# A router's softmax: one division for all eight heads at the end, and its loop of heads written out

## The reference, cut to what matters

```
sv, si = lax.top_k(s, PEER_TOPK)                       # 16 best of 128 keys, two halves per head
cand = sv[:, :, 0, :, None] + sv[:, :, 1, None, :]     # 256 candidate sums
cidx = si[:, :, 0, :, None] * N_KEYS + si[:, :, 1, None, :]
fv, fi = lax.top_k(cand.reshape(t, PEER_HEADS, 256), PEER_TOPK)
e = jnp.take_along_axis(cidx.reshape(t, PEER_HEADS, 256), fi, axis=-1)
g = jax.nn.softmax(fv, axis=-1)                        # over the 16 picks of a head
a = jax.nn.gelu(jnp.einsum('thkd,td->thk', peer_u[e], hb))
return jnp.einsum('thk,thkd->td', g * a, peer_v[e])
```

## Time and profile before

| what | us |
|---|---|
| three runs | 4075.23, 4058.43, 4070.72 |
| their median | 4070.72 |
| the profiled execution | 4065.13 |
| its span in the trace | 4063.3 |
| early router, VectorE's heads to its end | about 337 to 528 |
| late router, VectorE's heads to its end | about 1930 to 2238 |

### The profile page before, as it was taken

One profiled execution on the slowest core, in us unless ns is written; L12 is line 12 of the kernel. 1 busy time (PEld: TensorE's weight loads), 2 busy tenths in 40 slices (PEclk: granted clock), 3 DMA queues, 4 the chain that ended last, 5 costly groups with the idle time before them and its releaser, 6 DMA issues. The chain is left out here.

```text
span 4063.3 us, 57177 instructions
## 1 busy us (share of the span) xinstructions
PE 3284.5 (81%) x19892; PEld 2772.6 (68%) x19892; DVE 3008.0 (74%) x5897; ACT 1042.9 (26%) x1915; POOL 1648.1 (41%) x1320
## 2 busy tenths in 40 slices
PE   7665548787689889675663776999999999999997
PEld 4435424455455555334663666999999999999997
DVE  3316968678576777374998996888888888888886
ACT  2211112223122222111110553222232222222321
POOL 0004535346555655264455773333323333333232
PEclk9577779667787888777776888999999999999998
DMA  3032158468798887586100236888878888788786
GB/s 116 8 129 86 31 206 286 155 215 276 268 319 276 294 291 245 206 321 234 32 26 1 117 149 247 276 275 277 282 270 278 286 278 274 274 276 279 276 277 219
DMA packets 303822, 876.75 MB, mean 216 GB/s; under 512 B 34009, under 2 KB 125450, under 8 KB 292554
## 3 DMA queue, kind: packets, MB, share of 16 engines
q0 software_dynamic: 147456, 536.94, 39.0%
q1 hardware_dynamic: 154170, 334.15, 22.7%
q10 hardware_dynamic: 2016, 3.67, 0.2%
HBM read 819.17 MB, written 55.74 MB: 215 GB/s over the span
## 5 line engine op out<-in xcount | busy, mean ns | idle before, releaser
L109 POOL DMA_INDIRECT x_got<-v,x_expert x512 | 562.4, 1098 | 1062.9 <-DVE x_y L130 541.1
L109 POOL DMA_INDIRECT x_got<-u_rows,x_expert x512 | 613.8, 1199 | 659.8 <-DVE x_y L130 294.7
L130 DVE SCALAR_TENSOR_TENSOR x_y<-x_got,x_hidden,x_y 128x1024 f32<-128x1024 f32 x512 | 656.1, 1281 | 40.5 <-DMA x_got<-v,x_expert 38.0
L123 DVE SCALAR_TENSOR_TENSOR x_got<-x_got,x_y 128x1024 f32<-128x1024 f32 x512 | 626.7, 1237 | 43.8 <-DMA x_got<-u_rows,x_expert 42.2
L1667 PE MATMUL e_a<-h2h,e_uh 128*128 128x272 f32 x2048 | 590.4, 288 | 19.4 <-DVE e_ul L1745 19.4
L1669 PE MATMUL e_a<-h2h,e_ul 128*128 128x272 f32 x2048 | 594.0, 290 | 0.0
L1684 PE MATMUL e_y<-e_wh,e_vh 128*128 128x272 f32 x2048 | 588.9, 288 | 3.0 <-DVE e_wl L1768 3.0
L1668 PE MATMUL e_a<-h2l,e_uh 128*128 128x272 f32 x2048 | 589.2, 288 | 0.0
L1685 PE MATMUL e_y<-e_wl,e_vh 128*128 128x272 f32 x2048 | 588.7, 287 | 0.0
L1686 PE MATMUL e_y<-e_wh,e_vl 128*128 128x272 f32 x2048 | 587.7, 287 | 0.0
L1667 PEld LDWEIGHTS e_a<-h2h,e_uh 128*128 128x128 f32 x2048 | 386.3, 189 | 19.6 <-issue 19.6
(11 more groups left out here) (376 smaller groups left out, 5805.4 us busy)
## 6 DMA issues: line engine op xcount, KB each, us to landing
e_u<-uT SPq DMA_DIRECT2D x128, 512.0 KB
e_v<-v SPq DMA_DIRECT2D x64, 1024.0 KB
gates_d<-g_stage SPq DMA_DIRECT2D x8, 4352.0 KB
e_gate<-gates_d SPq DMA_DIRECT2D x32, 1088.0 KB
d_page<-page SPq DMA_DIRECT2D x128, 144.0 KB
d_latent<-page_rows SPq DMA_DIRECT2D x128, 128.0 KB
t0r_w<-w_pq SPq DMA_DIRECT2D x16, 512.0 KB
x_got<-u_rows,x_expert POOLq DMA_INDIRECT x512, 5.8
```

Of the source, the lines that this page charges most:

```text
L109: pool.indirect_dma_start(out=self.got[n % RING_G][:], out_offset=None, in_=self.tables[phase], in_offset=bass.IndirectOffsetOnAxis(ap=sel ...
L123: dve.scalar_tensor_tensor(out=row[:], in0=row[:], scalar=1.0, in1=self.y[g][:], op0=ALU.mult, op1=ALU.mult, accum_out=self.hidden[:, g, k ...
L130: dve.scalar_tensor_tensor(out=self.y[g][:], in0=row[:], scalar=self.hidden[:, g, k:k + 1], in1=self.y[g][:], op0=ALU.mult, op1=ALU.add).t ...
```

## The change

The exponentials go straight into their columns of `out[:, 0]` instead of back into `gate`. VectorE's `tail` of a head keeps only the sum, written to the head's column of a sum tile for all heads. The reciprocal and the product are done once, behind the last head, over all heads: 48 sums and 128x768 elements in the late router, 24 and 128x384 in the early one. The wait before L1446 is for the exponentials of the head before instead of its product; the waits for `c_gate` count to 1 instead of 8. In `heads` the hardware loop is replaced by a Python loop, so that each engine but SyncE has the code of all eight heads written out.

```diff
-        tot = sb("c_tot", [P, T])
-        inv = sb("c_inv", [P, T])
+        tot = sb("c_tot", [P, T, H])
...
             first(0, 0, None, False)
-            with eng.Fori(0, H // 2 - 1) as i:
-                first(2 * i + 1, 1, tail(2 * i, 0), False)
-                first(2 * i + 2, 0, tail(2 * i + 1, 1), False)
-            first(H - 1, 1, tail(H - 2, 0), True)
+            for m in range(1, H):
+                first(m, m % 2, tail(m - 1, (m - 1) % 2), m == H - 1)
             tail(H - 1, 1)()
...
-                    pe.wait_ge(s["c_gate"], H)
+                    pe.wait_ge(s["c_gate"], 1)
...
-                    act.activation(gate[:], gate[:], ACT.Exp).then_inc(s["c_exp"], 1)
+                    act.activation(out[:, 0, :, m * TOPK:(m + 1) * TOPK], gate[:], ACT.Exp).then_inc(s["c_exp"], 1)
...
-                after(dve, s["c_gate"], m)
+                after(dve, s["c_exp"], m)
...
                 dve.wait_ge(s["c_exp"], m + 1)
-                dve.tensor_reduce(tot[:], gate[:], AX, ALU.add).then_inc(s["c_tot"], 1)
-                dve.wait_ge(s["c_tot"], m + 1)
-                dve.reciprocal(inv[:], tot[:]).then_inc(s["c_inv"], 1)
-                dve.wait_ge(s["c_inv"], m + 1)
-                dve.tensor_tensor(out[:, 0, :, cols], gate[:], inv[:].unsqueeze(2).to_broadcast((P, T, TOPK)),
-                                  ALU.mult).then_inc(s["c_gate"], 1)
+                dve.tensor_reduce(tot[:, :, m:m + 1].rearrange("p t o -> p (t o)"), out[:, 0, :, m * TOPK:(m + 1) * TOPK], AX,
+                                  ALU.add).then_inc(s["c_tot"], 1)
             heads(dve, first, lambda m, e: lambda: None)
-            dve.wait_ge(s["c_gate"], H)
+            dve.wait_ge(s["c_tot"], H)
+            dve.reciprocal(tot[:], tot[:]).then_inc(s["c_inv"], 1)
+            dve.wait_ge(s["c_inv"], 1)
+            o4 = out[:, 0, :, :].rearrange("p t (h k) -> p t h k", h=H)
+            dve.tensor_tensor(o4, o4, tot[:].unsqueeze(3).to_broadcast((P, T, H, TOPK)), ALU.mult).then_inc(s["c_gate"], 1)
+            dve.wait_ge(s["c_gate"], 1)
```

## The result

The changed kernel took 4137.7 us (median of 6 runs, 4117.8 to 4149.5) against 4071.7 for the kernel before (6 runs): ratio 1.0166, 95% interval 1.0143 to 1.0189. The forecast was 4056.6, with a range of 4042 to 4074.

The account below looks back on a forecast made before the run. No engine fills the span; VectorE was taken to bound the late router, a ring through GpSimd, TensorE and ScalarE the early one. Gains 11.5 + 2.6 = 14.1 us: median 4070.72 to 4056.6, range 4042 to 4074.

Parts of the forecast that it names:

- Edits at no cost: Both routers: exponentials into `out`, the moved wait and TensorE's and ScalarE's written-out code add nothing to the sum.
- The slower rival: Routers: 12 heads leaving the loops each stall up to 2.3 us on late code, net 13.5 us slower, 4084.2; chance 0.08.
- The late router's sum: Late router: 9.2 us from heads 1 to 6, 3.2 from head 7, less 0.9 at the end: 11.5 us gained.
- The early router: Early router: 1.9 us from the written-out pick, 1.15 at head 7, less 0.5 for the product: 2.6 us gained.
- The forecast of the edit's own effect: Whole kernel: 14.1 us gained, median from 4070.72 to 4056.6 us, 0.35% less; chance 0.57.
- The cast isn't held: Late router: cast and split don't collide, scores set the period at 34.27; 18.6 us gained in all, 4052.1; chance 0.15.
- all of it comes back: Both routers: neither cast, scores nor early ring bind; 33 us gained, 4037.7; chance 0.07.
- the wait is inherited: Routers: the product's 2.7 us wait falls on VectorE's next instructions; only about 4 us gained, 4066.5; chance 0.13.
- I am wrong if ... the stages behind the routers change their lengths by more than the routers do: Sign against the forecast; its other signs: late period under 34.5 or over 36, or new idle time before L1403.

Follow-up runs that it names:

- e5: Kernel before with the heads written out on all engines but SyncE, softmax as before: 4150.8 us, ratio 1.0205.
- e1: The change with TensorE's heads kept in their hardware loop: 4049.8 us, ratio to the kernel before 0.9945.
- e3: The change with 50 extra transposes (100 instructions) on TensorE behind the late router's heads: 4043.3 us, ratio to the kernel before 0.9951.
- e7: Kernel before with 14 extra transposes (28 instructions) on TensorE behind the late router's heads: 4125.4 us, a single execution.

## Why the prediction was wrong, point by point

**The step that failed** is "Edits at no cost": "TensorE's and ScalarE's written-out code: both idle in the router". The cover was looked for in the router alone. The written-out heads cost TensorE nothing there; they moved the code behind them, and the experts loop, 38% of the span, came to lie across one block more. The term was set at 0 and is +89.0 us: 13 turns of 6.8. The trace takes them apart. In this stage a weight load mostly starts 0.125 us after the one before. Distances over 0.8 us, the waits, cost 62.7 us more than in the kernel before, 4.8 a turn; distances of 0.16 to 0.8 us cost 26.7 more, 2.1 a turn. The second kind is the lower clock: behind the second wait shown above, from 2999 to 3002 us, the loads start 0.227 us apart. From the end of the first of the two waits shown above, 10 us, and 10 us some 20 us on:

```profile
2994.00:3004.00 10.00, 7.31 (x44) 7.21 (x45) 5.77 (x7) 1.66 (x3) 2.23 (x2) 0.83 0.80 266
3014.00:3024.00 10.00, 10.00 (x82) 10.00 (x82) 8.05 (x13) 4.59 (x10) 0.94 (x1) 1.00 0.74 259
```

A mean of 0.83 says that for part of those 10 us the lower of the two levels, 1.2 instead of 2.4 GHz, was granted, behind two idle times of 1.9 and 2.3 us; then it is 1.00 again.

**The slower rival** had written-out code come in late, and so had the right kind of cause in the wrong place: it priced the twelve heads. In these no engine lost time: both routers got shorter. It was bounded by the longest wait of code that has no loop, but the row that would have told was one that counts instruction packets: 64 of them for a program of 65 blocks say that all of TensorE's loops stayed on the engine in the kernel before, and so that there was something to lose. The Trainium skill's "Runtime: NRT & Kernel Launch", section "Instruction fetch mechanics", was cited for its advice to write code out; its figures in the same section, 16 KiB blocks and 128 KiB for TensorE, were not set against a turn of 1598 instructions. The packets, 16384 bytes each, agree with the block. The trace of before disagrees with the section's note that a taken branch out of a window of two blocks fetches its target: this loop goes back over six blocks without a packet. An estimate from that section's 128 KiB, which are eight blocks: 7 and one fetched ahead would fit, 8 and one ahead would not. The 9 packets a turn are that count, but no run here shows the size of that memory.

**The late router's sum held**, step by step. GpSimd, one head to the next, and VectorE in between:

```profile
1997.75 4.95 POOL L1377 TENSOR_TENSOR t3c_eq<-t3c_eq,t3c_idf 128x1536 f32<-128x1536 f32 x1 [7.18 <-DVE t3c_eq L1455]
...
2013.96 2.34 POOL L1361 TENSOR_TENSOR t3r_wl<-t3r_w,t3r_wh 128x1024 fp32r<-128x1024 f32 x1
...
2032.63 4.95 POOL L1377 TENSOR_TENSOR t3c_eq<-t3c_eq,t3c_idf 128x1536 f32<-128x1536 f32 x1 [7.19 <-DVE t3c_eq L1455]
```

```profile
1999.25 0.25 DVE L1459 TENSOR_REDUCE t3c_tot<-t3c_out 128x6 f32<-128x96 f32 x1
1999.42 0.14 DVE L1400 COPY t3c_pad<-t3c_pad 128x1 f32<-128x1 f32 x1
...
2014.40 2.01 DVE L1435 CAST t3c_idf<-t3c_idx 128x192 f32<-128x192 uint32 x1
```

The period is 34.88 where 35.03 was forecast (36.56 before). The pad copy follows the sum in 0.17 us and takes 0.14, so the wait of the product is not handed down. The split begins 16.21 us after L1377 (forecast 16.2), the cast at 2014.40, 0.44 behind it, and takes 2.01 us where the earlier trace rows had 0.26: it sits the split out, to 2016.41, as did the early router's in the earlier trace rows. Heads 1 to 6 gained 10.4 us, forecast 9.2; head 7 gained 3.0 us (33.32 against 36.36), forecast 3.2. At the end, VectorE and GpSimd:

```profile
2207.27 0.45 DVE L1463 RECIPROCAL t3c_tot<-t3c_tot 128x48 f32<-128x48 f32 x1
2207.76 3.40 DVE L1466 TENSOR_TENSOR t3c_out<-t3c_out,t3c_tot 128x768 f32<-128x768 f32 x1
```

```profile
2205.48 4.86 POOL L1377 TENSOR_TENSOR t3c_eq<-t3c_eq,t3c_idf 128x1536 f32<-128x1536 f32 x1 [17.20 <-DVE t3c_eq L1455]
2210.42 4.03 POOL L1383 TENSOR_TENSOR t3c_eq<-t3c_eq 128x768 f32<-128x768 f32 x3
```

The product over all heads waits for L1377 to end at 2210.34 and itself ends at 2211.16: 0.82 us behind, forecast 0.85, and the three additions take 4.03 us instead of 3.43. From L1377 of the last head on, the router lost 0.5 us where 0.85 was put, and another 0.5 fell away ahead of the first pick, of which nothing was forecast. In all 13.5 us against 11.5.

**The early router** gave 4.9 us against 2.6. Its period went from 23.16 to 22.72, 0.44 a head where 0.3 was put; head 7 gained 1.10 (1.15 was put); the product cost less than put (additions 2.27 instead of 2.07); and about 1.5 us fell away ahead of the first pick, of which nothing was forecast. e5 had 2.9 of the 4.9, so most of it comes from writing the heads out.

**The other rivals.** "The cast isn't held" would have shown a period of 34.3, "all of it comes back" 33.3, "the wait is inherited" pad copies of 2 us or more: none did. "I am wrong if ... the stages behind the routers change their lengths by more than the routers do" is what happened. The forecast of the edit's own effect, 0.9965, lies inside the intervals of e1 and e3, 0.9945 and 0.9951, which are the change without the move of the experts loop onto a bad place.

## What to carry to other kernels

An edit that changes the number of instructions of an engine moves all loops behind it: compare the packets of the instruction queues, in all and per turn, before the stage's own lines are blamed. A loop whose turn is nearly as long as what stays on the engine should be kept shorter (an estimate from the counts above: with 61 instructions less this turn would touch 7 blocks from every place), or the count of instructions ahead of it chosen; here 100 instructions where TensorE waits anyway turned 1.7% slower into 0.5% faster. And a small product of 3 us on VectorE beside a GpSimd instruction is a wait: moved behind the last head it is paid once, though part of what it frees is spent at the next instruction that meets GpSimd.

## What the runs showed of the hardware that was not expected

- TensorE keeps a loop's turn of 1598 instructions over thirteen branches without a fetch, or fetches 9 packets of 16.4 KB in every turn, by its place alone: shifts of 0, 80 and 154 instructions keep it, 28 and 54 lose it. The second wait of a turn stands at the same place of a block from two beginnings 26 instructions apart; with a block beginning there, the turns that are kept touch 7 blocks and the others 8.
- A turn that is fetched anew costs 4.3 us (e7) to 6.8 us (the change), though its 9 packets are spread over 100 us and fill 0.6% of the DMA engines. What costs is the wait behind the branch back and, from 168, one more 26 instructions on (2.3 us each; in e7 one of 3.2), and the lower clock behind them, 2.1 us a turn in the change.
- VectorE's cast of 192 elements was held 1.75 us by a GpSimd instruction that had begun 0.44 us earlier; the pad copies of one element, 80 in each router, were never held (0.153 us in the late router, before and after).
